# Attention products of one decoder block at 128x128: scores over a pair of heads with zero-padded queries, values with the weight columns of both heads

## What is computed

```
def dilated_attention_group(q, k, v):          # 8 heads of 64 channels, 512 tokens
    qh, kh, vh = rotary(q), rotary(k), v        # split into heads
    for window, dilation in ((128, 1), (512, 4), (2048, 16)):
        scores = q_block @ k_blocks.T * 64 ** -0.5   # masked: causal, inside the window, on the dilation
        out, lse = softmax(scores) @ v_blocks, log_sum_exp(scores)
    weights = softmax(all lse)
    return sum(weights * outs)
```

## Time and profile before

| | us |
|---|---|
| median of three runs | 2100.16 |
| lowest and highest run | 2099.76 and 2102.77 |
| span of the profiled execution | 2101.9 |
| TensorE busy in it | 2068.7 (98%) |
| VectorE, ScalarE, GpSimd busy | 1548.5, 1136.2, 236.5 |
| attention, first scores to last values | 1573.0 to 1683.6 |

### The profile page before, as it was taken

How to read it: one execution, slowest core, us unless ns; L and a number is a source line. 1 busy time by engine, 2 the same in 40 slices (tenths; PEclk the granted TensorE clock), 3 DMA queues, 4 the chain that set the end, 5 groups by cost and what they waited for, 6 DMA issues and landing times.

```text
span 2101.9 us, 26301 instructions
## 1 busy us (share of the span) xinstructions
PE 2068.7 (98%) x9292; PEld 1625.5 (77%) x9292; DVE 1548.5 (74%) x1431; ACT 1136.2 (54%) x1054; POOL 236.5 (11%) x239
## 2 busy tenths in 40 slices
PE   8999999999999999999999999989999999999998
PEld 5864478888888888888888888858886668888887
DVE  6986399999999999999999999974773344333333
ACT  3132277777777777777777777753123523222222
POOL 0006211111111111111111111100000000000000
PEclk9999999999999999999999999999999999999999
DMA  5233399999999999999999999932221213222321
GB/s 224 91 140 126 135 402 394 395 384 379 381 381 383 381 381 381 382 380 381 380 384 378 383 379 384 361 132 80 71 90 61 81 41 111 99 85 97 121 80 40
DMA packets 79063, 522.31 MB, mean 248 GB/s; under 512 B 10353, under 2 KB 10881, under 8 KB 22049
## 3 DMA queue, kind: packets, MB, share of 16 engines
q1 hardware_dynamic: 66496, 483.88, 58.7%
q0 software_dynamic: 9056, 30.62, 5.7%
q10 hardware_dynamic: 3456, 7.06, 1.0%
HBM read 500.92 MB, written 18.60 MB: 247 GB/s over the span
## 4 chain that ended last, share of the span: by engine, by line
PE 94%; DVE 4%; ACT 1%; issue 1%; DMA 0%; DVEq 0%; SPq 0%; ACTq 0%
PE bank L1092 26%; PE bank L1094 26%; PE bank L1093 26%; PE bank L1084 5%; PE bank L1279 1%; PE bank L1428 1%; PE bank L1101 1%; PE bank L1488 1%; PE bank L1231 1%; PE bank L1507 1%; PE bank L1271 1%; PE bank L1130 1%; PE bank L1523 1%; PE bank L1497 1%; DMA ring<-in_wd 0%
## 5 line engine op out<-in xcount | busy, mean ns | idle before, releaser
L1830 DVE TENSOR_TENSOR ring_r<-ring,room_r 128x2048 fp32r<-128x2048 f32 x384 | 875.2, 2294 | 75.7 <-ACT room_r L749 69.7
L749 ACT ACTIVATE room_r<-ring 128x2048 fp32r<-128x2048 f32 x384 | 736.0, 1918 | 173.7 <-PE bank L1094 165.0
L1093 PE MATMUL bank<-ring_r,room_r 128*128 128x512 f32 x1744 | 679.0, 389 | 0.0
L1092 PE MATMUL bank<-room_r 128*128 128x512 f32 x1576 | 623.1, 395 | 2.4 <-DVE ring_r L1830 2.2
L1094 PE MATMUL bank<-room_r 128*128 128x512 f32 x1568 | 611.4, 390 | 0.0
L1093 PEld LDWEIGHTS bank<-ring_r,room_r 128*128 128x128 f32 x1744 | 327.7, 188 | 66.8 <-issue 1.7
L1092 PEld LDWEIGHTS bank<-room_r 128*128 128x128 f32 x1576 | 295.9, 188 | 65.5 <-DVE ring_r L1830 4.6
L1094 PEld LDWEIGHTS bank<-room_r 128*128 128x128 f32 x1568 | 294.3, 188 | 62.6
L1092 PE MATMUL bank<-room_r,ring_r 128*128 128x512 f32 x520 | 203.5, 391 | 1.8 <-DVE ring_r L1992 0.9
L1094 PE MATMUL bank<-room_r,ring_r 128*128 128x512 f32 x512 | 199.3, 389 | 0.0
L1093 PE MATMUL bank<-ring_r 128*128 128x512 f32 x384 | 149.5, 389 | 0.0
(11 more groups left out here) (289 smaller groups left out, 2133.0 us busy)
## 6 DMA issues: line engine op xcount, KB each, us to landing
ring<-in_wmoe SPq DMA_DIRECT2D x384, 1024.0 KB, 12.2
ring<-in_wf SPq DMA_DIRECT2D x33, 1024.0 KB, 4.8
ring<-in_wd SPq DMA_DIRECT2D x7, 2048.0 KB, 9.2
ring<-in_wp SPq DMA_DIRECT2D x14, 1024.0 KB, 5.0
ring<-in_wo SPq DMA_DIRECT2D x2, 2048.0 KB, 9.2
ring<-in_wd SPq DMA_DIRECT2D x2, 1024.0 KB, 8.8
room<-in_xtok ACTq DMA_DIRECT2D x1, 2048.0 KB, 12.7
h_rows<-room POOLq DMA_DIRECT2D x4, 512.0 KB, 3.0
```

The costliest lines, as they stand in the source:

```text
L749: act.activation(w_hi[s_ % PAIRS], raw_w[ORDER[s_]], ACT.Copy)\
L1092: pe.matmul(out, x_hi, w_hi, start=start, stop=False, skip_group_check=True)
L1093: pe.matmul(out, x_hi, w_lo, start=False, stop=False, skip_group_check=True)
L1830: dve.tensor_tensor(w_lo[i], raw_w[i], w_hi[s_ % PAIRS].bitcast(F32), ALU.subtract)\
```

## The change

TensorE's order stays what it was. The queries of the current head are copied by GpSimd into a tile of 128 partitions whose other 64 partitions are zero (`q_only`, one tile for even and one for odd heads). `scores` takes this tile as weights and all 128 partitions of the keys as the moving side; the other head's keys meet zeros. `values` takes the 128 columns of v of the head pair as weights, so its result has both heads on 128 partitions, of which one half is wanted; even heads write bank 4 and odd heads bank 5, and `head_out` reads the wanted half. A semaphore `q_ready` tells TensorE that a head's queries are copied, and the fifth output product, which uses bank 4, waits until head 6 has been read out of it.

```
+        q_only = [v(21760, S), v(9472, S)]
...
+            def head_queries(h):
+
+                lo = (h % 2) * DH
+                other = DH - lo
+                if h < 2:
+                    pool.wait_ge(s["rot_done"], 1 if h == 0 else 8)
+                    step(pool.memset(q_only[h][other:other + DH, :], 0.0))
+                else:
+                    pool.wait_ge(s["sc_ready"], TT * (h - 1))
+                pool.tensor_copy(q_only[h % 2][lo:lo + DH, :], qkT[lo:lo + DH, h // 2, :]).then_inc(s["q_ready"], 1)
+
+            for h in range(HEADS):
+                head_queries(h)
...
-                act.activation(mix_att[lo:lo + DH, h // 2, :], bank[5][lo:lo + DH, :], ACT.Copy)\
+                act.activation(mix_att[lo:lo + DH, h // 2, :], bank[4 + h % 2][lo:lo + DH, :], ACT.Copy)\
...
             def scores(u):
                 h, i = divmod(u, TT)
-                lo = (h % 2) * DH
-                m = h // 2
+                if i == 0:
+                    pe.wait_ge(s["q_ready"], h + 1)
                 if u >= 2:
                     pe.wait_ge(s["sc_done"], u - 1)
-                pe.matmul(bank[u % 2][:, 0:(i + 1) * P], qkT[lo:lo + DH, m, i * P:(i + 1) * P],
-                          qkT[lo:lo + DH, 4 + m, 0:(i + 1) * P], start=True, stop=True).then_inc(s["sc_ready"], 1)
+                pe.matmul(bank[u % 2][:, 0:(i + 1) * P], q_only[h % 2][:, i * P:(i + 1) * P],
+                          qkT[:, 4 + h // 2, 0:(i + 1) * P], start=True, stop=True).then_inc(s["sc_ready"], 1)
...
             def values(u):
-                lo = (h % 2) * DH
+                pair = h // 2 * P
...
-                    ins = pe.matmul(bank[5][lo:lo + DH, i * P:(i + 1) * P], v_tok[:, j, h * DH:(h + 1) * DH],
+                    ins = pe.matmul(bank[4 + h % 2][:, i * P:(i + 1) * P], v_tok[:, j, pair:pair + P],
                                     pTa[i][:, j * P:(j + 1) * P], start=(j == 0), stop=(j == i), skip_group_check=True)
...
             for g in range(2, 5):
                 if g == 2:
                     pe.wait_ge(s["pt_evac"], HEADS * TT)
+                elif g == 4:
+                    pe.wait_ge(s["pv_evac"], HEADS - 1)
                 w_out(g, 0, 3)
```

More of the change, by code:

```diff
@@ L365, in build @@
             out_ready out_written pool_waited dve_steps pool_steps moe_dve lb_ready
-            lbe_ready""".split()
+            lbe_ready q_ready""".split()
         s = {n: sem(n) for n in names}
```

## The result

| | before | changed |
|---|---|---|
| first set: median us (lowest to highest), runs | 2101.47 (2099.76 to 2103.24), 4 | 2086.38 (2083.13 to 2089.49), 4 |
| ratio, 95% interval | | 0.9916 (0.9896 to 0.9936) |
| second set, another time | 2103.28 (2102.09 to 2104.61), 7 | 2083.63 (2082.86 to 2085.96), 4 |
| ratio, 95% interval | | 0.9910 (0.9893 to 0.9926) |
| span of the first profiled execution | 2101.9 | 2081.7 |

What follows compares the result with a forecast made beforehand. TensorE was taken to bound the attention stretch: 119 changes of shape at 0.168 us make 20.0, less 1.1 of waits gives 18.9; from 2100.16 that is 2081 us, own range 2078 to 2084, eight in ten 2077 to 2088.

Steps and rivals of the forecast that it cites:

- The bound: From first scores to last values TensorE is busy throughout and sets the time; 94% of the span is TensorE.
- The sum over starts: One attention head: start-to-start pitches of its matmuls sum to 9.67 us against 12.36 measured, leaving 2.69 us of gaps.
- The price of a change: Each of 119 changes of matmul shape in attention costs 0.168 us, 20.0 us in all; bounds 13.3 and 21.4.
- The second stretch that I took for a check: Unit 22's scores to loop end: 24.45 us against pitches of 20.25, with 25 shape changes, again 0.168 each.
- The wider loads: Values load 128 weight columns, 192 ns instead of 136, hidden under matmuls: cost nothing; 9.0 us if uncovered.
- The copies: GpSimd's eight query copies and two memsets take 1.4 us each, and TensorE does not wait for them: 0 us.
- The new waits: TensorE waits 0.4 us for unit 7's last weight half and 0.75 at the first HGRN values; together 1.1 us.
- rival C: Other engines take over in the last ten units, 4.2 us more waits than none; 2085 us, chance 11%.
- A sign that was wrong: In the new profile, the first split product after a visit of scores lasts 0.39 us instead of 0.50.
- B: Rival: gaps at the transposes stay, so half the saving remains; 2091 us, a head of 11 us, chance 10%.
- E: Rival: gaps come from short products waiting on semaphores and stay, so nothing is gained; 2100 us, chance 3%.
- D: Rival: gaps stay and the values' wider weight loads come into the open, 9.0 us slower; 2109 us, chance 4%.

## Why the prediction was right

- *The bound.* TensorE sets the time of the stretch, and what left it left the kernel: 18.5 us of the stretch, and 0.0 given back in the 411.4 us behind it. Right.
- *The sum over starts.* 9.67 us was forecast for a head at one shape, 9.63 came. The pitches of 0.112, 0.43 and 0.23 from other places of the same trace, and the interpolated 0.218 and 0.324, were all it needed. Taking durations instead of starts would have shown a TensorE without gaps. Starts mislead too where a change of shape is near: the 0.056 us that I found between transposes and HGRN values at 1671.17 is the second part of the gap behind the values ahead of them, not a price of neighbours. So the lower bound of 0.11 for a change had no ground.
- *The price of a change.* 0.168 us was the mean over all 119. It holds for the sum because the change removes all of them; for a part it would have been off, as the runs with one half showed (expected 9.2 and 10.2, measured 10.3 and 8.5). The term is right in its sum and wrong in its kind: it goes with the load that follows. The second stretch that I took for a check, from 1652.50 to 1676.95, has 26 changes and not 25, so it gives 4.20/26 = 0.162 and not 0.168 again; there are more changes ahead of values and transposes in it, the cheaper ones.
- *The wider loads.* Costed at nothing and hidden: 191 ns each, and a head without a gap. There is an irony in it that the price explains: behind a change of shape a 64-column load cost more than a 128-column load that needs no change.
- *The copies.* Forecast 1.4 us each and no wait; 0.61 us, and the run without them has the same stretch.
- *The new waits.* 0.4 us in unit 7 and 0.75 at the first HGRN products; measured 0.50 and 0.78. Both were found by laying the other engines' chains beside TensorE's new pitches.
- *The sum.* 18.9 us forecast, 18.5 measured in the stretch; 17.7 and 18.9 by the two ratios, (1 - 0.9916) x 2101.5 and (1 - 0.9910) x 2103.3, each uncertain by some 4. The time itself, 2081, stood on a median of 2100.2 for the kernel before, whose later runs were at 2101 to 2105. The median of the first four runs, 2086.4, is outside the forecast's own range of 2078 to 2084, and within 2077 to 2088 only because that range had been widened for rival C, which was not what happened; that it lies within is luck in part. Two of the four runs had 2083 and two 2089; none of the next four was above 2086. The profiles of the two were not taken. Their mean granted clock was 0.994 and 0.995, against 0.996 and 0.997 of the other two; the execution with the first stretch of 253.9 us had 0.994 as well. So they probably lost the 6 us ahead of the first expert block, which is not shown.
- *A sign that was wrong.* I expected the split product behind the scores to be shown with 0.39 us instead of 0.50. It is shown with 0.58, for the reason given above.
- *Rivals.* B would have had 11 us a head, E 12.36, D more than that; the head of 9.63 excludes them. C had 4.2 us given back at the end of the loop; that piece shows 21.20 against a sum of 20.25, so 0.95, of which 0.78 is the wait at the first HGRN products. By its time alone, 2085, C would have fitted the first median better than the forecast; the stretches tell them apart.

## What to carry to other kernels

Look for matmuls of mixed forms in one stream. When each stands alone between others, padding small ones to the full array, with zeros on the contraction side or with columns nobody reads, can be worth more than it costs: here values of 128 columns of weights follow each other every 0.112 us, and those of 64 columns every 0.109. If a product can't be padded, put it where it shares a change of shape with another, and count for each change the weight load behind it. To find such gaps, sum the distances from start to start of the same forms elsewhere and compare with the length of the stretch. The busy share of TensorE and the durations of its matmuls will not show them. The idle time ahead of weight loads that is put down to "issue" is a hint: between 1571 and 1692 us, ahead of the first load of a split product, it was 10.1 us in 21 places before and 2.2 in 9 after.

## What the runs showed of the hardware

- A plain float32 weight load takes 108, 135 and 191 ns for 32, 64 and 128 columns, and the transposes' 140. At one shape the loads of 128 columns run under the matmuls, even with matmuls of 128 columns every 0.112 us. Behind a change of shape the next load begins about 0.09 us after the pitch of the last matmul is over, and the whole change costs that load plus 6 to 14 ns.
- This holds for every kind of change that was tried: rows (64\*128 and 128\*128), columns (128\*64 or 128\*32 and 128\*128), or both at once (128\*64 to 64\*128 in the run with scores first).
- Plain float32 products, split products and transposes can follow each other at no cost while the shape stays: a head with 20 + 10 + 8 + 18 matmuls in 16 pieces lasts 0.04 us less than the sum of their pitches.
- GpSimd copied 64 partitions of 512 float32 in 0.61 us, less than half of what I took from its nearest row.
